# The expert down-projection weights: issued behind ScalarE's loop over an expert's units, not by the sync engine

## The reference

```
g_idx   = argmax(xf @ w_group + b_group)                # one group of 8
top2    = top_k(expert logits inside that group, 2)
for each of 64 experts e, for the tokens routed to e:
    y = (silu(x @ w1[e]) * (x @ w3[e])) @ w2[e]         # w1, w3: 1024x512, w2: 512x1024
out[token] = sum over its two experts of weight * y
```

## Time and profile before

| | |
|---|---|
| median of 3 executions | 2650.03 us (2648.98 to 2650.74) |
| span of the profiled execution, first to last instruction | 2647.3 us |
| TensorE matmul busy | 2053.9 us, 78% |
| ScalarE busy | 272.4 us, 10% |
| DMA engines, from slice 23 to slice 38 of 40 | 90% or more in each |
| read from HBM, written | 481.17 MB, 35.95 MB |

### The profile page before, as it was taken

How to read it: one execution, slowest core, us unless ns; L and a number is a source line. 1 busy time by engine, 2 the same in 40 slices (tenths; PEclk the granted TensorE clock), 3 DMA queues, 4 the chain that set the end, 5 groups by cost and what they waited for, 6 DMA issues and landing times.

```text
span 2647.3 us, 25480 instructions
## 1 busy us (share of the span) xinstructions
PE 2053.9 (78%) x7526; PEld 933.2 (35%) x7527; DVE 471.0 (18%) x919; ACT 272.4 (10%) x488; POOL 210.7 (8%) x318
## 2 busy tenths in 40 slices
PE   6356789698999999989818887788777887777770
PEld 5245454544444444435402222223222232222220
DVE  3534211402111111112231010011000011000005
ACT  3000210111000000001100000000000011000001
POOL 1570000000000000000030000000000000000002
PEclk9655789899999999999959998899899999888895
DMA  7020321001022111031349999999999999999985
GB/s 244 0 62 0 119 72 52 0 10 46 1 56 51 36 36 36 32 123 64 114 133 325 356 353 358 361 357 354 361 355 362 360 349 358 360 363 357 363 307 194
DMA packets 404948, 518.86 MB, mean 196 GB/s; under 512 B 43712, under 2 KB 342752, under 8 KB 404384
## 3 DMA queue, kind: packets, MB, share of 16 engines
q1 hardware_dynamic: 382048, 456.45, 52.4%
q0 software_dynamic: 9888, 38.08, 4.5%
q10 hardware_dynamic: 12976, 23.87, 2.5%
HBM read 481.17 MB, written 35.95 MB: 195 GB/s over the span
## 4 chain that ended last, share of the span: by engine, by line
PE 44%; SPq 36%; DVE 8%; issue 5%; POOL 3%; ACT 2%; DMA 1%; POOLq 0%; ACTq 0%; DVEq 0%
SPq L446 34%; PE act_bank L660 21%; PE dve_bank L660 14%; PE act_bank L915 3%; DVE unit L1151 2%; SPq L449 2%; PE dve_bank L737 1%; SPq L484 1%; PE dve_bank L813 1%; PE act_bank L930 1%; POOL gain_a L533 1%; POOL gain_b L533 1%; DVE unit L1299 1%; ACT unit L961 1%; POOL unit_token_table L606 1%
## 5 line engine op out<-in xcount | busy, mean ns | idle before, releaser
L915 PE MATMUL act_bank<-unit,gain_a 128*64 128x512 f32 x1504 | 376.8, 659 | 88.9 <-DMA unit<-in_w 67.3
L660 PE MATMUL act_bank<-norm_store,unit 128*128 128x512 f32 x896 | 394.6, 595 | 9.3 <-DVE unit L1392 9.3
L930 PE MATMUL act_bank<-unit,rows_store 128*64 128x512 f32 x1168 | 266.7, 597 | 51.6 <-DVE rows_store L1539 51.6
L915 PE MATMUL act_bank<-mid_store,gain_a 128*64 128x512 f32 x832 | 209.0, 660 | 57.6 <-DMA mid_store<-in_w 46.3
L660 PEld LDWEIGHTS act_bank<-norm_store,unit 128*128 128x128 f32 x896 | 170.9, 191 | 224.5 <-issue 224.5
L915 PEld LDWEIGHTS act_bank<-unit,gain_a 128*64 128x64 f32 x1504 | 115.9, 151 | 314.9 <-issue 242.6
L660 PE MATMUL dve_bank<-unit 128*128 128x512 f32 (+1 forms) x576 | 219.1, 526 | 6.2 <-ACT unit L961 6.2
L1537 DVE TENSOR_TENSOR gain_a<-gain_a,act_bank 128x256 f32<-128x256 f32 x73 | 30.7, 421 | 712.8 <-ACT gain_a L1088 697.4
L930 PEld LDWEIGHTS act_bank<-unit,rows_store 128*64 128x64 f32 x1168 | 92.1, 136 | 179.4 <-issue 178.6
L660 PEld LDWEIGHTS dve_bank<-unit 128*128 128x128 f32 x576 | 101.6, 194 | 115.4 <-issue 107.2
L915 PEld LDWEIGHTS act_bank<-mid_store,gain_a 128*64 128x64 f32 x832 | 64.1, 151 | 183.1 <-issue 134.0
(11 more groups left out here) (202 smaller groups left out, 1373.7 us busy)
## 6 DMA issues: line engine op xcount, KB each, us to landing
unit<-in_w SPq DMA_DIRECT2D x688, 256.0 KB
unit<-in_w SPq DMA_DIRECT2D x64, 2048.0 KB
mid_store<-in_w SPq DMA_DIRECT2D x336, 256.0 KB
unit<-in_w_gate SPq DMA_DIRECT2D x24, 512.0 KB, 5.1
unit<-in_w_in SPq DMA_DIRECT2D x4, 2048.0 KB, 12.5
unit_results<-unit POOLq DMA_DIRECT2D x4, 2048.0 KB, 16.2
unit_results<-lane_row ACTq DMA_DIRECT2D x52, 128.0 KB
unit_results<-rows_store ACTq DMA_DIRECT2D x50, 128.0 KB
```

Source lines behind the costliest of these rows:

```text
L660: ins = nc.tensor.matmul(out_, stationary, moving, start=first and n == 0, stop=n == len(pairs) - 1)
L915: ins = nc.tensor.matmul(act_bank[0][h * CAP:(h + 1) * CAP, :], xT[:, k], w13[s][k // 4][:, k % 4, h].rearrange("p w n -> p (w n)"), start ...
L930: ins = nc.tensor.matmul(act_bank[1 + s][z * CAP:(z + 1) * CAP, :], hidT[:, j, h * CAP:(h + 1) * CAP], w2s[s][:, n, z * HALF:(z + 1) * HAL ...
```

## The change

SP no longer waits for `y_ready` in `refill` and no longer issues the down weights of experts 3 to 63. ScalarE issues the down weights of expert `e + 3` when it has finished its loop over the units of expert `e`, behind the stores of the last unit. The first three experts are loaded as before. The loop of ScalarE over the experts is written out for this: 20 turns of three experts, and the last four experts behind it.

```diff
             def refill(e, s):
                 first = sp.value_load(spans[0:1, 0, bass.ds(e, 1)], min_val=0, max_val=SLOT_UNITS)
-                up, down = expert(bass.ds(e, 1))
+                up, _ = expert(bass.ds(e, 1))
 
                 sp.wait_ge(per_slot["gu_ready"][s], first)
                 expert_up(up, s)
-                sp.wait_ge(per_slot["y_ready"][s], first)
-                expert_down(down, s)
...
-            each_unit(act, unit_work, numbered=True)
+            def expert_units(e, s):
...
+                with act.Fori(first, end) as c:
+                    unit_work(c, s, nc.s_assert_within(c + shift, 0, UNITS - 1, skip_runtime_bounds_check_because=(
+                        "the units of all experts are at most UNITS")))
+
+            def next_down(e, s):
+
+                act.dma_start(w2s[s], w2[0][bass.ds(e, 1)].rearrange("e (k p) n -> p (e k) n", p=P)
+                              ).then_inc(down_loaded[s], 16)
+
+            with act.Fori(0, E // SLOTS - 1) as t:
+                for s in range(SLOTS):
+                    expert_units(t * SLOTS + s, s)
+                    next_down(t * SLOTS + (s + SLOTS), s)
+            for e in range(E - SLOTS - 1, E):
+                expert_units(e, e % SLOTS)
+                if e + SLOTS < E:
+                    next_down(e + SLOTS, e % SLOTS)
```

More of the change, by code:

```diff
@@ L1096, in unit_work @@
                                   y_rows[s][z * CAP:(z + 1) * CAP]).then_inc(per_slot["y_stored"][s], 16)
-            each_unit(act, unit_work, numbered=True)
+            def expert_units(e, s):
+                at = bass.ds(e, 1)
+                first = act.value_load(spans[0:1, 0, at], min_val=0, max_val=SLOT_UNITS)
+                end = act.value_load(spans[0:1, 1, at], min_val=0, max_val=SLOT_UNITS)
+                shift = act.value_load(spans[0:1, 2, at], min_val=0, max_val=UNITS)
+                with act.Fori(first, end) as c:
[12 more added lines that the diff above has]
+                    next_down(e + SLOTS, e % SLOTS)
             for i in range(NT):
```

## The result

The changed kernel takes 2670.42 us (median of 4, 2668.53 to 2677.62), the kernel before 2649.51 (median of 4, 2647.88 to 2650.74): 20.9 us more, a ratio of 1.0084 with a 95% interval of 1.0069 to 1.0098. The profiled execution has a span of 2667.5 us, 20.2 over that of before.

A forecast was written before the change was run, and what follows sets the result against it. The prediction took the expert stage to be bound by the DMA transfer of weights. Its terms, 11.1 + 2.8 + 5.2 + 2.3 - 3.0, summed to +18.4 us, giving 2668.4, with 2652 to 2692 for 8 in 10.

The forecast's parts named there:

- start, down(3) earlier: From 1393.5 to 1406: ScalarE issues down(3) some 6 us earlier, beside up(3), filling the DMA window; -3.0 us.
- experts 18 and 19: Two units each: down loads moved earlier leave a DMA gap of 0.2 to 5.4 us; taken as +2.8.
- experts 37 to 39: Two, one and three units: without two or three down loads DMA stands still 8.5 to 13.7 us; taken as +11.1.
- end: up weights last: At the stage's end up(63) is moved last instead of down(63), so up matmuls start behind all weights; +5.2 us.
- end: TensorE's last unit: Last up loads take 12.0 us each, less than TensorE's 14.34 for a unit, so the last unit starts later; +2.3 us.
- The surplus of 1.9 us: Experts 37 to 39, kernel before: 83.9 us of DMA work against the 82.0 for which DMA must be fed.
- The rate, taken as unchanged: Expert stage: two queues would not change the DMA rate; term zero, bounded by 402 and 318 GB/s.
- rival (c): Down loads among up weights get 318 GB/s, costing 6.6 instead of 5.2 us each; 2753 or some 2700 us; chance 0.10.
- Rival (e): ScalarE stops at its issue, so silu comes late and TensorE's stretches lose +10 more; 2680 us; chance 0.03.
- Rival (a): Only the ends count: a full q1 keeps DMA fed through both stretches; +4.5, 2654.5 us; chance 0.15.
- (d): Hidden anyway: DMA is full, order doesn't matter, start and end cancel; 2650 us, as before; chance 0.05.
- (b): Faster: two queues hide the cost of small pieces, up pieces going at 402 GB/s; 2640 us; chance 0.09.

The follow-up runs named there:

- e6: The kernel before, but ScalarE issues down(3) alone and all others stay with SP; 2650.01 against 2648.50 us, ratio 1.0005.
- e3: The kernel before, but ScalarE issues only the down loads of experts 3 to 32, 30 of 61; 2650.93 against 2648.85 us.
- e4: The kernel before, but ScalarE issues only the down loads of experts 33 to 44, 12 of 61; 2656.77 against 2648.85 us.
- e9: The changed kernel, but ScalarE issues each down load one expert later; 2666.66 us against 2648.13 for the kernel before.
- e1: The kernel before, all weights on SP's queue, but from expert 4 on down weights are issued ahead of up weights; 2661.89 against 2648.85 us.
- e5: The kernel before, but ScalarE issues only the down loads of experts 45 to 63, 19 of 61; 2656.80 against 2648.50 us.
- e2: The changed kernel, but the down loads of experts 61 to 63 go back to SP; 2663.26 us against 2648.85 for the kernel before.
- e7: The kernel before, with w1 and w3 laid out in SBUF so that up loads come in 2 KB pieces; 2580.62 against 2648.50 us.
- e11: The kernel before, with up loads as 4 DMAs of 1 MB in pieces of 8 KB; 2551.75 against 2648.13 us.

## Why the prediction was right, step by step

The forecast was +18.4 us; it is +20.9. Its own terms against the trace and the runs:

| term | forecast | measured |
|---|---|---|
| start, down(3) earlier | -3.0 | -1.7 at equal bytes; by itself (e6) not seen in the time |
| experts 18 and 19 | +2.8 | +1.8 at equal bytes, but with no gap, and not repeated by e3 |
| from there to 260 MB | 0 | +1.0 at equal bytes |
| experts 37 to 39 | +11.1 | +8.3 at equal bytes, up(42) 10.5 later; e4 +7.9 |
| slow drift, from 275 to 420 MB | 0 | +2.9 at equal bytes |
| end: up weights last | +5.2 | +5.0 |
| end: TensorE's last unit | +2.3 | +3.3 |

The measured terms add up to 20.6, the 20.5 us by which the last unit starts later. That the forecast came within 2.5 us of the result is in part luck: the gap was taken 2.8 too large, and that hides most of the 3.9 of slow loss that it had at nothing.

**DMA bounds the stage, and the order of service decides.** Shown: e3 makes nothing of half the loads, e4 has the gap with a fifth of them, e9 keeps it with the same count of down loads left, and e1 has one on a single queue, though with a later issue of up(42) in it. The surplus of 1.9 us by which the kernel before kept DMA fed was the number on which the forecast stood, and it held.

**Size of the gap.** Forecast as 8.5 to 13.7 us of standstill. The windows give 15.5 us at 190 GB/s where 350 could flow, 15.5 x (1 - 190/350) = 7.1, and a weak restart; the lag grows by 8.3. It is the lower end, 8.5, that of two down loads missing: ScalarE's rows have three of the five left for the stretch, those of 39, 40 and 41. I had taken the middle, where the count could have been made: down(39) is issued when expert 36 is done, which is when the stretch begins.

**Experts 18 and 19.** The step that failed as put: I expected a gap of up to 5.4 us. There is none; from 1750 to 1775 the DMA share is 1.07 at 329 GB/s. SP does wait for TensorE there, 5.7 us in all, but its queues hold enough to keep DMA busy. Lag is lost, if at all, by a lower rate, and e3, where the term should stand alone, has none of it left at 200 MB. That the number came near is luck.

**The end.** Right in kind, and the second half was mis-sized. DMA is done with the weights at 2582.6 (the share from 2576 to 2584 is 0.81, from 2584 to 2592 it is 0.14). That is 17.3 behind the last up weights of the kernel before: 12.3 of lag and 5.0 of order. The last unit starts 3.9 us behind it, where it was 0.6 before: TensorE adds 3.3. I had counted a unit as 14.34 us, but the one before the last had waited and ran its up matmuls in 8.66 us instead of 7.09, which makes the unit 15.8.

**The rate, taken as unchanged.** Nearly so. With both weight loads in flight DMA moves 397 GB/s, as the two alone would, mostly down weights in this window. The rule of the Trainium skill ("DMA: Bandwidth & Descriptors", "Issuing engines are not separate DMA queues") is borne out: a second issuer brought no bandwidth. But over 310 us of single units the rate is 357 against 360 GB/s, 0.8% or 2.6 us. This is the drift, a term that I put at nothing. The same window of e5 and of e1:

```profile
2230.00:2540.00 310.00, 220.02 (x928) 75.10 (x928) 24.59 (x48) 15.68 (x32) 16.98 (x31) 0.86 1.07 357
```

```profile
2230.00:2540.00 310.00, 229.16 (x958) 77.80 (x954) 26.12 (x51) 24.38 (x40) 17.52 (x32) 0.87 1.08 362
```

It is 356 in e2 too, and 360 to 362 in e3, e4 and e6. So wherever ScalarE issues the down loads of this stretch the rate is lower, and e1, with another order on one queue, isn't slower: the drift goes with the second queue, a small part of rival (c). From 1410 to 1700 there is no such difference, 359 in both kernels. What makes it stays open; no run here takes it apart.

**ScalarE's issues cost nothing.** An issue takes 0.395 us, and silu starts at 2159.76 behind up matmuls that end at 2159.73. Rival (e) is out by the trace; no run was made for it alone. Rival (a) is out by the gap, (d) by the time. (b) asked for a stage rate over 365 GB/s and (c) for one under 350 outside the gaps: it is 354 with the gap in it and 357 beyond, so both are out, but for the 0.8% above.

## What to carry to other kernels

When a stage is bound by transfers, look at the one stretch in which the computing engine keeps the buffers longest, and count the transfers that can still be made in it: the order of service that leaves most of them for that stretch wins, even though the bytes and the buffers are the same. Here transfers in the order of their need did this by themselves; a second queue for a part of them broke it, and it also decided what was moved last. And when an engine's queue heads the chain of waits, ask for the size of its pieces before its order: here moving the loads cost 21 us, and larger pieces gained 96.

## What the hardware showed that I had not expected

The two queues didn't share by bytes. While a down load (4 KB packets, q10) runs beside up weights (1 KB packets, q1), the packets counted from 2132 to 2136 carry some 320 GB/s of down and 76 of up weights, 4.2 to 1, about one packet against one; over all 305 us of the trace in which nothing but these two is in flight it is 0.8 down packets to one of up weights. Still a down load takes 12.7 us from issue to landing, with 5.2 us of DMA work in it:

```profile
DMA to landing us min/median/max: 11.2/12.7/15.9
```

The time of a piece was nearly linear in its size: 349 GB/s at 1 KB and 402 at 4 KB gave an estimate of 383 for 2 KB, and the packets of e7 show 383 to 389 in stretches of up weights alone. For 8 KB the same line gives 412; in such stretches of e11 it is mostly 414 to 426.

TensorE's clock adds to a wait. In the changed kernel the 32 up matmuls take 7.09 us at a granted clock of 1.00 (2.4 GHz), and 8.4 to 10.1 us in the 34 cases from 1400 us on where TensorE had stood for 2.4 us or more before them; in the window from 2572 to 2576, just behind such a wait, the granted clock is 0.76. At the end of the stage this decides whether a lead is kept: e3 and e6 reach the last unit 0.5 and 1.5 us ahead and then spend 2.6 and 3.0 us more on its up matmuls than the kernel before.
